# Evictions ahead of the next weight preparation in a two-layer hybrid decoder kernel

## The reference

```
for layer in range(2):
    h = rms_norm(x, norm_g)
    proj = h @ w_in                              # 1024 x 10696, cut into ten parts
    y_a = latent attention(q_lat, kv_lat)        # low-rank q and kv, rotary key part
    y_b = gated DeltaNet(dn_qkv, dn_a, dn_b)     # short conv, chunked delta rule, chunks of 64
    y_c = dilated attention(dil_qkv)             # three head groups, merged by denominators
    ys  = [y_a * silu(z_a), y_b * silu(z_b), y_c * silu(z_c)]
    branch_out = ys @ w_branch
    mixed = sum(sigmoid(gate_logits) * branch_out)
    x = x + mixed @ w_out
```

## Time and profile before

| | |
|---|---|
| median of the runs | 886.16 us (3 runs, 880.74 to 886.27) |
| the profiled execution | 886.54 us, span 884.8 us |
| TensorE busy | 853.0 us, 96% of the span |
| VectorE busy | 596.4 us, 67% |
| ScalarE busy | 501.0 us, 57% |
| GpSimd busy | 271.7 us, 31% |
| mean granted TensorE clock | 0.985 |
| DMA | 124.40 MB, 141 GB/s |

### The profile page before, as it was taken

One profiled execution on the slowest core, in us unless ns is written; L12 is line 12 of the kernel. 1 busy time (PEld: TensorE's weight loads), 2 busy tenths in 40 slices (PEclk: granted clock), 3 DMA queues, 4 the chain that ended last, 5 costly groups with the idle time before them and its releaser, 6 DMA issues.

```text
span 884.8 us, 12226 instructions
## 1 busy us (share of the span) xinstructions
PE 853.0 (96%) x4588; PEld 735.0 (83%) x4588; DVE 596.4 (67%) x764; ACT 501.0 (57%) x1035; POOL 271.7 (31%) x249
## 2 busy tenths in 40 slices
PE   6989999899999999999999899989999999999998
PEld 6877888778888888888898678878788888888886
DVE  4478769786656368485665885797675755775754
ACT  6686466437557455345468666555574755544542
POOL 1245012592515001251122610256543330114130
PEclk9899999999999999999999999999999999999999
DMA  8444435352533344457465344453434243454551
GB/s 254 150 150 165 139 113 160 112 143 74 147 113 120 119 142 143 144 153 227 132 189 158 105 149 133 129 157 105 131 108 139 86 158 96 140 157 154 172 197 61
DMA packets 69826, 124.40 MB, mean 141 GB/s; under 512 B 7181, under 2 KB 14343, under 8 KB 69639
## 3 DMA queue, kind: packets, MB, share of 16 engines
q1 hardware_dynamic: 69200, 122.37, 45.1%
q10 hardware_dynamic: 567, 1.24, 0.4%
HBM read 122.55 MB, written 1.05 MB: 140 GB/s over the span
## 4 chain that ended last, share of the span: by engine, by line
PE 74%; DVE 10%; POOL 6%; ACT 6%; issue 2%; DMA 1%; POOLq 0%; ACTq 0%; SPq 0%; DVEq 0%
PE bank L665 18%; PE bank L667 18%; PE bank L666 18%; DVE w_lo L1212 3%; PE bank L797 2%; PE bank L751 2%; PE bank L869 2%; PE bank L861 2%; ACT w_hi L963 2%; PE bank L868 2%; PE bank L769 2%; PE bank L695 1%; POOL sm L1588 1%; DVE at L1407 1%; ACT at L1034 1%
## 5 line engine op out<-in xcount | busy, mean ns | idle before, releaser
L1212 DVE TENSOR_TENSOR w_lo<-raw,w_hi 128x1024 fp32r<-128x1024 f32 (+4 forms) x240 | 311.1, 1335 | 107.1 <-ACT w_hi L963 105.9
L665 PE MATMUL bank<-w_hi,hT 128*128 128x512 f32 (+2 forms) x800 | 318.9, 399 | 11.9 <-ACT at L1041 10.6
L667 PE MATMUL bank<-w_hi,hT 128*128 128x512 f32 (+2 forms) x800 | 310.4, 388 | 0.0
L666 PE MATMUL bank<-w_lo,hT 128*128 128x512 f32 (+2 forms) x800 | 310.3, 388 | 0.0
L963 ACT ACTIVATE w_hi<-raw 128x1024 fp32r<-128x1024 f32 (+4 forms) x240 | 233.6, 1016 | 60.7 <-PE bank L667 56.8
L665 PEld LDWEIGHTS bank<-w_hi,hT 128*128 128x128 f32 x800 | 152.6, 191 | 43.8 <-ACT at L1041 12.2
L667 PEld LDWEIGHTS bank<-w_hi,hT 128*128 128x128 f32 x800 | 151.9, 190 | 30.1
L666 PEld LDWEIGHTS bank<-w_lo,hT 128*128 128x128 f32 x800 | 152.5, 191 | 26.6
L1588 POOL TENSOR_TENSOR sm<-sm,tab 128x8 f32<-128x8 f32 (+2 forms) x72 | 65.2, 906 | 252.1 <-ACT at L1041 105.2
L1162 ACT ACTIVATE at<-at,sm 128x128 f32<-128x128 f32 (+1 forms) x64 | 32.8, 514 | 65.1 <-DVE sm L1440 51.8
L665 PE MATMUL bank<-w_hi,yT 128*128 128x512 f32 (+1 forms) x136 | 54.0, 397 | 0.2
(11 more groups left out here) (210 smaller groups left out, 1123.7 us busy)
## 6 DMA issues: line engine op xcount, KB each, us to landing
raw<-in_w_in SPq DMA_DIRECT2D x168, 512.0 KB, 4.1
raw<-in_w_branch SPq DMA_DIRECT2D x24, 512.0 KB, 3.8
raw<-in_w_out SPq DMA_DIRECT2D x16, 512.0 KB, 4.5
raw<-in_w_in SPq DMA_DIRECT2D x8, 384.0 KB, 5.9
raw<-in_w_in SPq DMA_DIRECT2D x8, 320.0 KB, 4.3
raw<-in_mla_w_kv_b SPq DMA_DIRECT2D x8, 256.0 KB, 2.8
raw<-in_mla_w_q_b SPq DMA_DIRECT2D x4, 384.0 KB, 3.3
tab<-in_tables ACTq DMA_DIRECT2D x1, 1152.0 KB, 9.5
```

The lines of the kernel that those rows point to most:

```text
L665: mm(o, src[0][:, a, tok], hi[:, k, :], start=starts and p == k == 0, stop=False)
L666: mm(o, src[0][:, a, tok], lo[:, k, :], start=False, stop=False)
L667: last = mm(o, src[1][:, a, tok], hi[:, k, :], start=False, stop=ends(u, p) and k == k1 - k0 - 1)
L1212: tt(view(w_lo, q % SPLIT, k1 - k0, n), view(raw, q % RAW, k1 - k0, n), view(w_hi, q % SPLIT, k1 - k0, n).bitcast(F32), ALU.subtract).then ...
```

## The change

In the order list the eviction of a unit moves ahead of the preparation of piece 2u + 4. TensorE's work is in the same order as before, since neither entry has a TensorE part. On ScalarE the entries trade places in the units that it evicts, 27 of the 60 of a layer; on VectorE in z, branch and out units; in the other units of those that end a sum, VectorE has no part in the eviction, and its order is as before. Units that end no sum are as before.

```diff
             order += [(layer, s) for s in middle.get(u, [])]
             order.append((layer, ("unit", u, 1)))
-            order += ahead(layer, u, 0)
             if whole(u) or UNITS[u][2] == 1:
                 order.append((layer, evict_step(u)))
+            order += ahead(layer, u, 0)
             order += [(layer, s) for s in steps[u]]
             order += ahead(layer, u, 1)
```

## The result

The changed kernel takes 935.88 us (median of 4 runs, 934.98 to 936.83) against 886.21 us before: a ratio of 1.0571, 95% interval 1.0532 to 1.0610. The forecast was 937 us with a range of 905 to 960. The profiled execution has a span of 933.2 us, 48.4 more than before.

The account below looks back on a forecast made before the run. TensorE, busy 96% of the span, was taken as the bound, so new waits add in full. Site losses of 22.3 us a layer (44.6) plus 6 for the clock on 886.5 gave 937 us, range 905 to 960.

Parts of the forecast that it names:

- Unit 8, 4.6 us: Units 6 to 8: VectorE's taps start late, so piece 17 reaches TensorE late without slack; 4.6 us a layer.
- Unit 12, 3.6: Units 11 and 12: taps and `k_rs` run late and the transposes wait for them; 3.6 us a layer.
- Units 17 to 21, 4.0: VectorE 4.5 us late, little made up before `dn_kk`; loss 3.3 to 4.5, taken as 4.0 us a layer.
- Unit 22, 3.5: VectorE takes up `dn_kk` late, and `dn_qk`'s second half waits for the bank it frees; 3.5 us a layer.
- Unit 26, 4.1: VectorE is late at step 26, where two rounds of `dn_TX` share the same two banks; 4.1 us a layer.
- Unit 33, 2.0: Units 32 and 33: late softmax delays a copy TensorE uses; 4.1 late less 2.4 slack, taken as 2.0 us a layer.
- What it wins, 0: Shorter eviction wait at latkv, up to 1.06 us a layer, taken as cancelled by late small tiles at unit 3.
- The other ending units, 0.5 a layer: Remaining sum-ending units start no VectorE work TensorE soon needs, or ScalarE's copy stays; 0.5 us a layer, between 0 and 3.
- The queues: SyncE's raw-piece loads issue up to 4.6 us later but are covered by two units of matmuls; costed at nothing.
- The clock: TensorE runs at 1.2 GHz for a while behind each new wait; 0 to 12 us in all, taken as 6.
- The one in which slack swallows the delay: Rival: prepared slots hide the delay, piece 17 is ready by 60.78 and eviction waits shrink; 876 us, chance 0.04.
- The smaller loss of 24 us: Rival: steps catch up, only units 6, 11 and 17 count, where TensorE already waited; 911 us, chance 0.2.

Follow-up runs that it names:

- the six units: Eviction first only in units 6, 11, 17, 22, 26 and 32 of each layer, against the kernel before: 929.96 us, ratio 1.0523.
- all but the six units moved: Eviction first in every sum-ending unit except 6, 11, 17, 22, 26 and 32, against the kernel before: 896.24 us, ratio 1.0138.
- unit 6 alone: Eviction first only in unit 6 (the first qb unit) of each layer, against the kernel before: 889.85 us, ratio 1.0059.
- With TensorE kept busy: Changed kernel plus unused TensorE products in its waits at steps 22 and 26: 928.66 us, ratio 1.0491 to the kernel before.
- The unused work in the kernel before: Kernel before plus unused TensorE products ahead of unit 8 and in steps 21 and 25: 882.15 us, ratio 0.9961.

## Why the prediction was right

The mechanism held as it was put: nothing is added, the copy of piece 2u + 4 moves behind the end of the unit, VectorE stands at the low part with its steps behind it, and TensorE pays where a step has no slack. The comparison of VectorE's list (low part ahead of the steps or behind them, 42 us apart) shows the queue; the six units (46 of 50 us) show the places.

*Unit 8, 4.6 us.* Confirmed: the wait for piece 17 is 3.9 us where it was 0.24, and the six matmuls of unit 8 ahead of it ran slower than before; lag 5.1 with the clock, 4.8 with that unit alone. *Unit 12, 3.6.* The wait is 3.4 us where 0.2 was before; lag 6.0, since the clock fell behind it. The stretch from 97 to 99 us, TensorE, with the columns as above:

```profile
97.00:99.00 2.00, 2.00 (x11) 0.50 0.32 31
```

*Units 17 to 21, 4.0.* The waits came to 3.3 us, the lower end of the term: 1.9 us for the bank of the transposed keys, 0.3 for the eviction of the branch unit (line 1231) and 1.1 more on `dn_kk`; the rest of the lag of 4.5 is clock. None was for the weights of units 19 and 20. That unit 17 is what made `dn_kk` late is not shown: with all but the six units moved that wait grew as much (7.6 us in two), and with the six alone not at all (5.3), where TensorE waited 1.4 us for the branch eviction instead. *Unit 22, 3.5.* The wait is 3.3. *Unit 26, 4.1.* The wait is 4.6, and the clock behind it, 2.5 us of its own, was not in this term. *Unit 33, 2.0.* 1.8, of it a wait of 1.3 for the copy on line 1146, which is the step that I named.

*What it wins, 0.* In layer 0 the lag is -1.3 us ahead of unit 8, but it is -1.4 there with unit 6 alone, where unit 1 has the old order, so this is no win that can be told. Of the 3.5 us by which the waits for line 1041 are shorter, 1.9 are at latkv, nearly all of it in layer 0, where that wait differed by as much as a microsecond between executions with the old order. The other 1.6 are at the kvb evictions; these waits are gone with the six units alone too, though unit 10 was not moved there. Alone the move at latkv could not be told from nothing (0.9994).

*The other ending units, 0.5 a layer.* Near enough in the changed kernel, but not for the reason given. The other units cost 12 us by themselves; most of that is covered by the six.

*The queues.* Right at the size that mattered. ScalarE's waits for loads of raw pieces are 8.8 us in all, where 3.8 were before, and none of TensorE's waits is for one. *Low parts beside GpSimd* hardly mattered: the longest took 2.9 us, against 3.4 before, and all of them together 8.3 us more.

*The sum.* Its total was right to 1.1 us, its two parts were not. The sites were put at 44.6 us and the clock at 6. New waits, and what the old ones grew by, are 41.0 us, but TensorE's idle time grew by 32.0 only, because 9 us of old waits went away (3.9 for GpSimd on line 1711, 3.5 on line 1041, 1.6 on line 1407); and the matmuls took 16.9 us longer, nearly three times the term and above the upper end of 12 that I gave it. Two errors of 13 and 11 us of opposite sign met, so that the total came within 1.1 us is luck.

*The clock.* Its direction was right (0.962 for 0.985), its price was not. I had read 1.2 us from five matmuls behind the wait that ended at 60.78. The rows of the kernel before show that the clock had fallen ahead of that wait, and that the wait to look at is the one of 1.96 us at the start of the unit:

```profile
58.60 0.50 PE L665 MATMUL bank<-w_hi,hT 128*128 128x512 f32 x1 [1.96 <-ACT at L1041]
...
59.91 0.63 PE L667 MATMUL bank<-w_hi,hT 128*128 128x512 f32 x1
```

Nor did the slow stretches stay as short as that. As the clock has two levels, a mean of 0.985 over 884.8 us means some 27 us at 1.2 GHz, and 0.962 over 933.2 us some 71, waits included (an estimate). The Trainium skill (TensorE: Matmul & The Clock Gate, What's actually happening) has the ramp at less than 1% of a typical span. It says so of a kernel's first matmuls; here the slow ones lie behind waits all through the kernel, the added time alone is 1.8% of the span, and that figure is no bound for it.

*The rivals.* The one in which slack swallows the delay, with the Trainium skill's "Evacuate promptly" (PSUM — Partial Sum Buffer, Summary: rules for kernel authors) beside it, fell at the point that was named: piece 17 was ready after TensorE wanted it. The Trainium skill gives the smallness of that memory as its reason and promises no time; here TensorE waited for evictions for 10.6 us of 884.8, and the change that followed the rule lost 5.7%. The smaller loss of 24 us fell at units 22 and 26, whose waits are 3.3 and 4.6 us.

*The -3.6 us at unit 26* were in no term. With TensorE kept busy the wait for GpSimd stayed whole (1.96 us in layer 0) and 1.6 came back, and it was the same with the six units alone. So 2.0 of the 3.6 are the wait that went away, and 1.6 are the clock, which in the kernel before was slow behind that wait. The unused work in the kernel before took the same 1.6 us off there.

## What to carry to other kernels

Where all engines walk one list, an entry costs its duration only on the engine that does it; on an engine that waits for it, it costs from the time at which its input comes. So for a moved step, take the end of its new input, add the step, and compare with the start of what is queued behind it, engine by engine. Losses found in this way don't add up where one engine is late already; and behind a new wait of TensorE a slower clock can be a term of its own: here 1.6 us behind a wait of 3.3, and 2.5 behind one of 4.6. It is not a fixed price. With the six units alone the clock was 1.00 from 189 to 193 us, behind the same wait of 3.3 us, and in the changed kernel the 1.6 us were taken up by the wait for GpSimd that would have come next.

## What was not expected of the hardware

Work that nothing uses, put in two waits a layer, took 7.2 us off the changed kernel; put in three waits of the kernel before, 4 us (0.9961, 0.9945 to 0.9976). In the profiled run with it the clock was 0.998 on average, 0.985 before.

Slow stretches differ between executions. Unit 10 took 4.6 us in layer 1 of the kernel before, and 3.0 in layer 0 and in the changed kernel. In the steps ahead of it there was a wait of 1.4 us on line 1407, against 0.2 and none. But a wait of that length doesn't decide it: with unused work it was there in both layers, and unit 10 took 3.0 us in both; with the eviction first in unit 1 besides, the wait was the same and unit 10 took 4.6 in both. The time of single runs goes with the granted clock. Of the twelve runs of the kernel before with unused work, the two with a clock of 0.998 took 878.5 and 878.8 us, and the three with 0.990 took 884.2 to 884.5. The kernel before itself spread from 880.5 to 888.0 us. What sets off such a stretch in one execution and not in the next is not shown.
